# Two of GpSimd's weight differences put behind VectorE's short chains, alpha moved into the mix's addition, and experts 0 and 1 written out of the loop

## The chip, the cores and the metric

The program runs on one NeuronCore of one Trainium2 chip. The time is device microseconds (us) of that core, from the start to the end of the program on the chip. The kernel before was timed three times on its own: 1068.28 us is the median (1068.08 to 1070.03). A change is called faster or slower in this document only where it moves the median by over 0.2%.

## The reference

Two post-norm layers act on 512 tokens of 1024 channels in fp32. Each layer is a mix and a mixture of experts:

```
x <- LN(alpha * x + Mix(x))     # conv 256 channels | attention, 8 heads, chunks of 64 | gated MLP 256
x <- LN(alpha * x + MoE(x))     # 16 experts, 2 per token, SwiGLU of 512

h   = x @ w_in + b_in                                     # 1792 columns
c   = silu(LN(causal_conv31(a * sigmoid(g))))
att = softmax over the own and the previous chunk of 64 keys, with a learned sink per head
gm  = u * (masked 128x128 mixing of LN(v)) ,  u, v = gelu(h[...])
Mix = concat(c, att, gm) @ w_out + b_out
MoE = sum over the two chosen experts e of gate_e * (silu(x @ w_gate[e]) * (x @ w_up[e])) @ w_down[e]
```

alpha is (2 * 2) ** 0.25, the same number in both layers.

## The kernel before, in words

Every weight and every activation that TensorE multiplies is split into two numbers of TensorE's fast fp32 format, a high part and a low part, and each product is three matmuls: high by high, low by high and high by low. ScalarE makes the high part of a weight (a copy into `wh`), and VectorE or GpSimd makes the low part (`wl` = raw weight minus `wh`).

**The mix.** The weights of the mix come in 11 pieces a layer. Pieces 0 to 6 are the columns of `w_in`, pieces 7 to 10 are `w_out`. A piece is loaded by SyncE into one of two raw buffers, then ScalarE's `piece` (line 893) writes its high part into one of three slots, then a low part follows. Pieces 2 to 9 have their lows on GpSimd (`piece_lows`, line 1607), piece 10 on VectorE (line 1142). Piece 10's low part is the one that TensorE needs last, in the middle of `out_second`. SyncE loads piece q only when the low part of piece q - 2 is done, so a late low part also makes a late load.

VectorE meanwhile computes the convolution as 62 taps (line 1173), with the rotary products between them (`rope`, lines 1148 to 1150), then masks the score banks (line 1493), and then runs four short softmax chains, one for each block of 128 tokens: `softmax_max` (lines 1191 to 1197) before ScalarE's exponentials (lines 987 and 989), `softmax_norm` (lines 1204 to 1206) behind them. The probabilities are normalised in `Pm`, and TensorE turns them (`turn_probs`, line 597), scores the next block (`scores`, line 577) and multiplies by the values (`attend`, line 612). The order on each engine is written out by hand, and each waits for the others by semaphores, instruction by instruction.

GpSimd's queue in the mix is, in this order: the lows of pieces 2 to 7, a clear and two small transfers for the values (lines 1697 to 1699), four multiplications of the token-major input `xtok` by alpha (line 1706), the two powers for the norms (lines 1709 and 1711), the gated MLP's norm (line 1716), the lows of pieces 8 and 9, and four additions of `b_out` to `xtok` (line 1723). After that VectorE adds the projection to `xtok` (`add_mix`, line 1266) and takes the norm's sums.

**The experts.** The tokens are routed on the chip into chunks of 128 slots, one or more for each expert. TensorE runs one loop over all chunks. ScalarE, VectorE and GpSimd need to know which of the two weight buffers a chunk uses, so they run a loop over eight pairs of experts, and in it a loop for the chunks of each of the two (`chunk_loops`, lines 267 to 275). Each pass of the outer loop reads the experts' first chunks into registers (`first_chunk`, line 256). VectorE enters it right after `late_out` (line 1423), which waits for TensorE's `late_tables`. In every chunk VectorE first makes low parts of the gathered tokens (`gathered_low`, line 1142 with `xTl`), and then those of the first half of the gate weights; TensorE's `widen` (line 776) waits for both. `narrow` (line 794) is the down projection.

## Time and profile before

| | |
|---|---|
| median of three timed runs | 1068.28 us (1068.08 to 1070.03) |
| the profiled execution's own time | 1068.19 us |
| its span, first to last instruction | 1066.3 us |
| PE busy | 985.3 us (92%) |
| DVE busy | 809.4 us (76%) |
| ACT busy | 655.1 us (61%) |
| POOL busy | 539.8 us (51%) |
| chain that ended last | PE 69%, DVE 21%, issue 3%, POOL 2%, ACT 2% |
| mean over the DMA engines | 252 GB/s |

PE is TensorE, DVE VectorE, ACT ScalarE, POOL GpSimd and SP SyncE. The span has five parts: the first mix up to about 180 us, routing to 205, the experts of layer 0 to 525, the second mix to 720, and from 744 on the experts of layer 1 and the last norm. In the profile's lines "idle before" names what the engine waited for. PEclk is the share of full speed that TensorE was granted: 1.00 is 2.4 GHz, 0.50 is 1.2 GHz.

### The profile page before, as it was taken

How to read it: one execution, taken by the hardware profiler on the slowest of the kernel's cores; microseconds unless marked ns; L12 is line 12 of the kernel's file. 1: busy time of each engine (PE TensorE's matmuls, PEld its weight loads, DVE VectorE, ACT ScalarE, POOL GpSimd, SP SyncE). 2: the span in 40 equal slices, each digit the busy share in tenths (PEclk: the TensorE clock that was granted, in tenths of full speed). 3: DMA queues.
4: the chain of work that ended last, by engine and by line, in shares of the span. 5: the costliest groups of instructions: out<-in, count | busy, mean ns of one | idle time of the engine just before them, and what ended most of it. 6: DMA issues, size and time to landing. Idle time of an engine off the chain costs nothing.

```text
span 1066.3 us, 15510 instructions
## 1 busy us (share of the span) xinstructions
PE 985.3 (92%) x4852; PEld 792.6 (74%) x4852; DVE 809.4 (76%) x967; ACT 655.1 (61%) x737; POOL 539.8 (51%) x291
## 2 busy tenths in 40 slices
PE   7989998599999999999999979995999999999995
PEld 5876777488888888877778757774788888888882
DVE  5996757777878787777878977476877777777876
ACT  5324823377888787777533346323788787887861
POOL 1635354246566665545425354540656565656553
PEclk9998999599999999999999999996899999999998
DMA  9634293399999999995813211733999999999962
GB/s 291 222 89 174 69 335 125 134 318 354 359 346 367 342 333 342 354 344 174 251 53 119 79 49 40 291 143 116 324 372 362 360 365 360 356 362 333 368 218 82
DMA packets 122304, 268.51 MB, mean 252 GB/s; under 512 B 10523, under 2 KB 26043, under 8 KB 121760
## 3 DMA queue, kind: packets, MB, share of 16 engines
q1 hardware_dynamic: 111136, 247.14, 64.3%
q0 software_dynamic: 11136, 20.96, 7.4%
q8 instruction: 18, 0.29, 0.1%
q14 instruction: 14, 0.11, 0.0%
HBM read 259.19 MB, written 27.79 MB: 269 GB/s over the span
## 4 chain that ended last, share of the span: by engine, by line
PE 69%; DVE 21%; issue 3%; POOL 2%; ACT 2%; DVEq 1%; DMA 0%; SPq 0%; ACTq 0%
PE bank L776 34%; PE bank L794 17%; PE bank L431 9%; DVE bank L1173 7%; PE bank L754 2%; DVE xTl L1142 2%; POOL xtok L1621 1%; PE bank L748 1%; DVE moemem L1429 1%; DVE w_gate L1149 1%; PE bank L577 1%; DVE small L1194 1%; PE bank L829 1%; PE bank L825 1%; PE bank L544 1%
## 5 line engine op out<-in xcount | busy, mean ns | idle before, releaser
L1675 POOL TENSOR_TENSOR wl<-w_down,wh 128x2048 fp32r<-128x2048 f32 x33 | 151.8, 4601 | 148.8 <-ACT wh L1041 148.8
L1142 DVE TENSOR_TENSOR wl<-w_gate,wh 128x2048 fp32r<-128x2048 f32 (+1 forms) x75 | 169.5, 2260 | 53.1 <-ACT wh L1041 35.9
L1142 DVE TENSOR_TENSOR wl<-w_up,wh 128x2048 fp32r<-128x2048 f32 x66 | 151.2, 2293 | 29.2 <-ACT wh L1041 28.4
L1041 ACT ACTIVATE wh<-w_up 128x2048 fp32r<-128x2048 f32 x66 | 126.6, 1918 | 31.7 <-PE bank L794 21.7
L1041 ACT ACTIVATE wh<-w_down 128x2048 fp32r<-128x2048 f32 x66 | 126.7, 1920 | 31.0 <-PE bank L776 29.0
L776 PE MATMUL bank<-wl,xTh 128*128 128x512 f32 x528 | 144.0, 395 | 1.6 <-DVE wl L1142 1.6
L776 PE MATMUL bank<-wh,xTl 128*128 128x512 f32 x528 | 144.0, 395 | 1.1 <-DVE xTl L1142 1.1
L776 PE MATMUL bank<-wh,xTh 128*128 128x512 f32 x528 | 144.5, 396 | 0.2 <-ACT wh L1041 0.2
L1607 POOL TENSOR_TENSOR wl<-w_gate,wh 128x2048 fp32r<-128x2048 f32 x16 | 73.6, 4606 | 123.1 <-ACT wh L893 122.8
L1041 ACT ACTIVATE wh<-w_gate 128x2048 fp32r<-128x2048 f32 x66 | 126.5, 1916 | 12.8 <-PE bank L794 8.8
L1142 DVE TENSOR_TENSOR xTl<-bank,xTh 128x512 fp32r<-128x512 f32 (+1 forms) x168 | 89.8, 574 | 44.9 <-issue 21.4
L776 PEld LDWEIGHTS bank<-wl,xTh 128*128 128x128 f32 x528 | 100.1, 191 | 24.4 <-DVE wl L1142 3.9
L776 PEld LDWEIGHTS bank<-wh,xTl 128*128 128x128 f32 x528 | 100.6, 191 | 23.4 <-DVE xTl L1142 2.5
L776 PEld LDWEIGHTS bank<-wh,xTh 128*128 128x128 f32 x528 | 101.1, 192 | 21.7 <-issue 0.5
L431 PE MATMUL bank<-xTh,wh 128*128 128x512 f32 (+1 forms) x256 | 102.6, 401 | 11.2 <-DVE xTl L1142 9.8
L1654 POOL DMA_INDIRECT moemem<-x_rows,gather_idx x33 | 83.2, 2522 | 28.9 <-POOL gather_idx L1648 28.9
L431 PE MATMUL bank<-xTl,wh 128*128 128x512 f32 (+1 forms) x256 | 96.0, 375 | 0.0
L431 PE MATMUL bank<-xTh,wl 128*128 128x512 f32 (+1 forms) x256 | 95.9, 374 | 0.0
L1662 POOL DMA_INDIRECT y_rows<-moemem,scatter_idx x33 | 62.0, 1878 | 46.9 <-issue 46.9
L1142 DVE TENSOR_TENSOR wl<-w_down,wh 128x2048 fp32r<-128x2048 f32 x33 | 75.7, 2293 | 9.2 <-ACT wh L1041 8.3
L1173 DVE SCALAR_TENSOR_TENSOR bank<-w_down,col,bank 128x512 f32<-128x512 f32 x116 | 77.7, 748 | 1.7 <-DVE w_down L1157 0.5
L1045 ACT ACTIVATE xTh<-bank 128x512 fp32r<-128x512 f32 x66 | 39.1, 593 | 63.5 <-PE bank L748 63.5
(228 smaller groups left out, 1796.7 us busy)
## 6 DMA issues: line engine op xcount, KB each, us to landing
w_up<-in_exp_w_up SPq DMA_DIRECT2D x32, 2048.0 KB, 18.4
w_down<-in_exp_w_down SPq DMA_DIRECT2D x32, 2048.0 KB, 17.7
w_gate<-in_exp_w_gate SPq DMA_DIRECT2D x32, 2048.0 KB, 17.6
w_gate<-in_w_in SPq DMA_DIRECT2D x13, 1024.0 KB, 5.6
w_gate<-in_w_out SPq DMA_DIRECT2D x8, 1024.0 KB, 5.0
y_rows<-moemem SPq DMA_DIRECT2D x8, 512.0 KB, 9.4
x_rows<-xtok POOLq DMA_DIRECT2D x8, 512.0 KB, 3.0
w_up<-y_rows SPq DMA_DIRECT2D x8, 512.0 KB, 4.7
```

The lines of the kernel that those rows point to most:

```text
L431: mm = pe.matmul(out, xs[i], ws[k], start=(first and n == 0), stop=(last and n == 2))
L754: mm = pe.transpose(bank[4 + 3 * i][:, P * (k % 2):P * (k % 2) + P], sg[:, P * k:P * k + P], ident)
L776: mm = pe.matmul(bank[piece][:, :], xgT[m][:, 4 * (i % 2) + k, :], w[q][:, k, :], start=(i % 2 == 0 and n == 0 and k == 0), stop=(i % 2 == ...
L794: mm = pe.matmul(bank[5 + n][:, :], heT[m][:, 2 * (i % 2) + k, :], w[q][:, k, 512 * n:512 * n + 512], start=(i == 4 and t == 0 and k == 0) ...
L1041: act.activation(wh[s][:, :], slot[r][p][:, cols], ACT.Copy).then_inc(half_high, 1)
L1045: act.activation(xgT[0][:, 4 * i:4 * i + 4, :], bank[2 + i][:, :].rearrange("p (k t) -> p k t", k=4), ACT.Copy).then_inc(xgT_high, 1)
L1142: return dve.tensor_tensor(out, src, high.bitcast(F32), ALU.subtract)
L1173: y = dve.scalar_tensor_tensor(o, x, wk, o, ALU.mult, ALU.add)
L1607: pool.tensor_tensor(wl[(n + l) % SLOTS][:, :], wraw[n % 2], wh[(n + l) % SLOTS][:, :].bitcast(F32), ALU.subtract)\
L1654: pool.indirect_dma_start(xg, None, x1d[l], bass.IndirectOffsetOnAxis(ap=rows[:, :], axis=0), bounds_check=T - 1, oob_is_err=False).then_i ...
L1662: pool.indirect_dma_start(yd[l], bass.IndirectOffsetOnAxis(ap=scatter_idx[:, :], axis=0), ysb, None, bounds_check=T - 1, oob_is_err=False, ...
L1675: pool.tensor_tensor(wl[s][:, :], slot[r][p][:, cols], wh[s][:, :].bitcast(F32), ALU.subtract)\
```

## The change

There are three edits, all in the order or the form of instructions; TensorE's and SyncE's programs stay as they were.

1. GpSimd waits for `mask_set` (VectorE has masked the score banks) before the low part of piece 7, and for the second block's `pn_done` (its probabilities are normalised) before the low part of piece 8.
2. The four multiplications by alpha are gone. VectorE's `add_mix` computes x * alpha + projection in one instruction. So that `b_out` keeps its weight, GpSimd multiplies the row of `b_out` by 1 / alpha once, before its four additions.
3. `chunk_loops` runs experts 0 and 1 ahead of the loop over pairs, which starts at pair 1. The three first chunks are read before `late_out`'s wait on VectorE, and before the waits for the tables on GpSimd.

```diff
-        def chunk_loops(eng, l, body):
-
-            with eng.Fori(0, E // 2) as pair:
+        def chunk_loops(eng, l, body, ready=None):
+
+            starts = [first_chunk(eng, l, e) for e in range(3)]
+            if ready:
+                ready()
+            for r in range(2):
+                with eng.Fori(starts[r], starts[r + 1]) as c:
+                    body(c, 0, r)
+            with eng.Fori(1, E // 2) as pair:
...
-                link(dve.tensor_tensor(x, x, bank[4 * n + j][:, :], ALU.add))
+                link(dve.scalar_tensor_tensor(x, x, ALPHA, bank[4 * n + j][:, :], ALU.mult, ALU.add))
...
-                late_out(l)
-                chunk_loops(dve, l, lambda c, pair, r: chunk(l, c, pair, r))
+                dve.wait_ge(start_set, l + 1)
+                chunk_loops(dve, l, lambda c, pair, r: chunk(l, c, pair, r), lambda: late_out(l))
...
+                pool.wait_ge(mask_set, l + 1)
                 piece_lows(l, 7)
...
-                if l == 0:
-                    pool.wait_ge(xtok_in, 16)
-                else:
-                    pool.wait_ge(tr_done, TT * 2 * l)
-                for j in range(TT):
-                    link(pool.tensor_scalar(xtok[:, j, :], xtok[:, j, :], ALPHA, None, ALU.mult))
...
+                pool.wait_ge(pn_done, TT * l + 2)
                 piece_lows(l, 8)
                 piece_lows(l, 9)

                 pool.wait_ge(rows_in, 32 * l + 16)
+                link(pool.tensor_scalar(rows3[:, 0, :], rows3[:, 0, :], 1.0 / ALPHA, None, ALU.mult))
+                if l == 0:
+                    pool.wait_ge(xtok_in, 16)
+                else:
+                    pool.wait_ge(tr_done, TT * 2 * l)
                 for j in range(TT):
                     pool.tensor_tensor(xtok[:, j, :], xtok[:, j, :], rows3[:, 0, :], ALU.add).then_inc(xb_done, 1)
...
-                pool.wait_ge(tab_set, l + 1)
-                pool.wait_ge(late_set, l + 1)
-                chunk_loops(pool, l, lambda c, pair, r: chunk(l, c, r))
+
+                def tables():
+                    pool.wait_ge(tab_set, l + 1)
+                    pool.wait_ge(late_set, l + 1)
+
+                chunk_loops(pool, l, lambda c, pair, r: chunk(l, c, r), tables)
```

GpSimd in the mix of layer 0, before: the lows of pieces 3 to 7 (`wl<-w_gate,wh`), the values' transfers, alpha, the powers, the gated MLP's norm and the low of piece 8.

```order
L1607 TENSOR_TENSOR wl<-w_gate,wh 128x2048 [waits piece_high] x5
L1697 MEMSET w_down 64x128 [waits v_set]
L1698 DMA w_down<-w_down 64x512 [waits pool_chain]
L1699 DMA w_down<-w_down 64x384
L1706 TENSOR_SCALAR xtok<-xtok 128x1024 [waits xtok_in]
L1706 TENSOR_SCALAR xtok<-xtok 128x1024 [waits pool_chain] x3
L1709 TENSOR_TENSOR small<-small 128x4 [waits cvar_set,pool_chain]
L1711 TENSOR_TENSOR small<-small 128x4 [waits gvar_set]
L1716 TENSOR_TENSOR w_gate<-w_gate,w_down 128x1024 [waits row_in,gvh_set]
L1716 TENSOR_TENSOR w_gate<-w_gate,w_down 128x1024 [waits pool_chain]
L1607 TENSOR_TENSOR wl<-w_gate,wh 128x2048 [waits pool_chain,piece_high]
```

The same stretch of GpSimd's queue in the changed kernel:

```order
L1613 TENSOR_TENSOR wl<-w_gate,wh 128x2048 [waits piece_high] x4
L1613 TENSOR_TENSOR wl<-w_gate,wh 128x2048 [waits piece_high,mask_set]
L1704 MEMSET w_down 64x128 [waits v_set]
L1705 DMA w_down<-w_down 64x512 [waits pool_chain]
L1706 DMA w_down<-w_down 64x384
L1709 TENSOR_TENSOR small<-small 128x4 [waits cvar_set]
L1711 TENSOR_TENSOR small<-small 128x4 [waits gvar_set]
L1716 TENSOR_TENSOR w_gate<-w_gate,w_down 128x1024 [waits row_in,gvh_set]
L1716 TENSOR_TENSOR w_gate<-w_gate,w_down 128x1024 [waits pool_chain]
L1613 TENSOR_TENSOR wl<-w_gate,wh 128x2048 [waits pool_chain,piece_high,pn_done]
```

The four alpha instructions are out of it, and two lows have one more semaphore each. Further on in the same queue, the low of piece 9 and what follows it, before:

```order
L1607 TENSOR_TENSOR wl<-w_gate,wh 128x2048 [waits piece_high]
L1723 TENSOR_TENSOR xtok<-xtok,w_gate 128x1024 [waits rows_in]
L1723 TENSOR_TENSOR xtok<-xtok,w_gate 128x1024 x3
L1616 TENSOR_TENSOR small<-small 128x1 [waits ln_var]
L1621 TENSOR_TENSOR xtok<-xtok,w_gate 128x1024 [waits ln_scaled]
```

The same in the changed kernel, where `w_gate<-w_gate` is the row of `b_out`, scaled:

```order
L1613 TENSOR_TENSOR wl<-w_gate,wh 128x2048 [waits piece_high]
L1723 TENSOR_SCALAR w_gate<-w_gate 128x1024 [waits rows_in]
L1729 TENSOR_TENSOR xtok<-xtok,w_gate 128x1024 [waits xtok_in,pool_chain]
L1729 TENSOR_TENSOR xtok<-xtok,w_gate 128x1024 x3
L1622 TENSOR_TENSOR small<-small 128x1 [waits ln_var]
L1627 TENSOR_TENSOR xtok<-xtok,w_gate 128x1024 [waits ln_scaled]
```

One instruction has come in between the low of piece 9 and the additions. VectorE at the entry to layer 0's experts, before (`gatef` is what `late_out` writes, `starti` holds the first chunks):

```order
L1423 TENSOR_REDUCE gatef<-bank 128x48 [waits late_done]
L269 UNCONDITIONAL_BRANCH
L269 ISA
L256 TENSOR_LOAD starti
L256 ISA x3
L256 TENSOR_LOAD starti
L256 ISA x2
L274 UNCONDITIONAL_BRANCH
L274 ISA
L1142 TENSOR_TENSOR xTl<-bank,xTh 128x512 [waits xgT_high]
```

And in the changed kernel:

```order
L256 TENSOR_LOAD starti [waits start_set]
L256 ISA x2
L256 TENSOR_LOAD starti
L256 ISA x2
L256 TENSOR_LOAD starti
L256 ISA x2
L1429 TENSOR_REDUCE gatef<-bank 128x48 [waits late_done]
L273 UNCONDITIONAL_BRANCH
L273 ISA
L1148 TENSOR_TENSOR xTl<-bank,xTh 128x512 [waits xgT_high]
```

The reads of the first chunks now stand ahead of the wait, and one loop's entry is left behind it.

## Rows read from the trace of the kernel before

**Rows 1.** The chain that ended last, layer 0 experts and layer 1 mix: start us, us.
```profile
248.36 10.90 PE bank L776 x48
...
650.93 4.18 DVE small L1194
```

**Rows 2.** VectorE by time, layer 0 mix: start us, us, engine, line, operation [idle before].
```profile
68.41 0.69 DVE L1149 TENSOR_TENSOR w_gate<-w_gate,w_down 128x512 f32<-128x512 f32 x1
...
74.66 0.90 DVE L1149 TENSOR_TENSOR w_gate<-w_gate,w_down 128x512 f32<-128x512 f32 x1
...
89.69 0.84 DVE L1204 TENSOR_TENSOR small<-small 128x8 f32<-128x8 f32 x1 [1.61 <-ACT w_up L989]
...
96.16 0.17 DVE L1194 SCALAR_TENSOR_TENSOR small<-small,col 128x8 f32<-128x8 f32 x1
...
111.56 4.20 DVE L1194 SCALAR_TENSOR_TENSOR small<-small,col 128x8 f32<-128x8 f32 x1
...
143.94 0.28 DVE L1142 TENSOR_TENSOR wrs<-moemem,wrs 128x128 fp32r<-128x128 f32 x1
...
149.07 4.27 DVE L1142 TENSOR_TENSOR wl<-w_gate,wh 128x2048 fp32r<-128x2048 f32 x1 [4.85 <-ACT wh L893]
```

**Rows 3.** ScalarE by time around the third block's softmax.
```profile
113.40 1.28 ACT L987 ACT_TABLE_LOAD   x1
...
116.12 0.21 ACT L987 ACTIVATE small<-small 128x8 f32<-128x8 f32 x1 [1.44 <-DVEq L1198]
```

**Rows 4.** TensorE by time, layer 0 mix.
```profile
117.90 1.10 PE L597 MATMUL bank<-cst,w_up 128*128 128x128 f32 x8 [1.15 <-DVE w_up L1206]
...
119.17 2.56 PE L577 MATMUL bank<-w_gate 64*64 64x128 f32 x32 [0.17 <-ACT w_up L989]
...
155.02 0.39 PE L431 MATMUL bank<-wh,xTh 128*128 128x512 f32 x1
```

**Rows 5.** GpSimd by time, layer 0 mix.
```profile
70.40 4.61 POOL L1607 TENSOR_TENSOR wl<-w_gate,wh 128x2048 fp32r<-128x2048 f32 x1 [8.09 <-ACT wh L893]
...
83.69 11.40 POOL L1706 TENSOR_SCALAR xtok<-xtok 128x1024 f32<-128x1024 f32 x4
...
111.12 4.61 POOL L1607 TENSOR_TENSOR wl<-w_gate,wh 128x2048 fp32r<-128x2048 f32 x1 [0.18 <-POOL w_gate L1716]
...
141.62 2.38 POOL L1723 TENSOR_TENSOR xtok<-xtok,w_gate 128x1024 f32<-128x1024 f32 x1
...
143.96 2.52 POOL L1723 TENSOR_TENSOR xtok<-xtok,w_gate 128x1024 f32<-128x1024 f32 x1
...
148.80 2.39 POOL L1723 TENSOR_TENSOR xtok<-xtok,w_gate 128x1024 f32<-128x1024 f32 x1
```

**Rows 6.** VectorE by time: an addition with a product, and a plain one.
```profile
20.75 0.75 DVE L1157 SCALAR_TENSOR_TENSOR w_down<-bank,col,w_down 128x512 f32<-128x512 f32 x1 [1.07 <-PE bank L431]
...
175.17 0.69 DVE L1266 TENSOR_TENSOR xtok<-xtok,bank 128x512 f32<-128x512 f32 x1 [1.57 <-PE bank L431]
```

**Rows 7.** VectorE by time: first experts of layers 0 and 1.
```profile
206.96 1.35 DVE L1142 TENSOR_TENSOR xTl<-bank,xTh 128x512 fp32r<-128x512 f32 x3 [1.80 <-issue]
...
224.02 1.35 DVE L1142 TENSOR_TENSOR xTl<-bank,xTh 128x512 fp32r<-128x512 f32 x3 [0.37 <-ACT xTh L1045]
...
243.27 1.35 DVE L1142 TENSOR_TENSOR xTl<-bank,xTh 128x512 fp32r<-128x512 f32 x3 [1.40 <-issue]
...
745.96 1.35 DVE L1142 TENSOR_TENSOR xTl<-bank,xTh 128x512 fp32r<-128x512 f32 x3 [1.53 <-issue]
```

**Rows 8.** TensorE by time, first chunk of layer 0.
```profile
207.71 2.08 PE L776 MATMUL bank<-wh,xTl 128*128 128x512 f32 x4 [0.70 <-DVE xTl L1142]
...
210.57 2.08 PE L776 MATMUL bank<-wl,xTh 128*128 128x512 f32 x4 [0.79 <-DVE wl L1142]
```

**Rows 9.** One stretch: us, busy (x) PE PEld DVE ACT POOL, PEclk, DMA, GB/s.
```profile
189.30:216.50 27.20, 17.45 (x64) 13.58 (x65) 20.34 (x53) 10.10 (x10) 7.09 (x4) 0.50 0.32 107
```

**Rows 10.** ScalarE by time, a late expert of layer 0.
```profile
465.25 1.92 ACT L1041 ACTIVATE wh<-w_gate 128x2048 fp32r<-128x2048 f32 x1 [1.95 <-DMA w_gate<-in_exp_w_gate]
```

## The prediction

> **What bounds the kernel now.** I read the chain of waits first, then the engines' rows in order of time at the three places that the change touches. TensorE carries 69% of the chain, mostly the experts, where its matmuls follow each other without a gap: 48 of them take 10.90 us, 0.227 us each [rows 1]. Nothing in the change makes those shorter. What can move is where the chain leaves TensorE. In the mix of each layer it goes through a scalar_tensor_tensor of VectorE on 128x8 numbers that takes 4.20 us in layer 0 and 4.18 us in layer 1 [rows 1, 2]; elsewhere the same instruction takes 0.17 us [rows 2]. It begins at 111.56, 0.44 us after GpSimd's low part of piece 8 (111.12, 4.61 us) and ends when that ends, at 115.73 [rows 5]. At the entry to the experts, TensorE waits 0.70 and 0.79 us for VectorE, which itself stood 1.80 us for no semaphore [rows 7, 8].
>
> **Edit 1, the low part of piece 8.** With it behind the second block's probabilities, VectorE's 4.20 us become 0.17, and its small instructions up to the normalised probabilities are 4.03 us earlier. TensorE doesn't get all of that. ScalarE is the next to be late: its exponentials of the third block began at 116.12 after a wait of 1.44 us, and the table load in front of them ends at 113.40 + 1.28 = 114.68 [rows 3]. So they can start 1.42 us earlier. TensorE's turn of block 1 waited 1.15 us for VectorE, and its scores of the last block waited for ScalarE [rows 4]; the latter now come 1.42 us earlier, and all that follows hangs on these two. Gain 1.42 us a layer, bounds 1.15 (if only TensorE's first wait goes) and 4.03. The moved low begins at about 117.90 - 4.03 = 113.9 and ends at 118.5. The next instructions of VectorE wait for ScalarE, which is free only when the exponentials end, just before the scores, now at 119.17 - 1.42 = 117.75; two of them read PSUM and come first, so by the time two operands in SBUF are read the low has ended, and I count nothing there. If this cover fails, what comes back is at most the overlap, under 1 us. SyncE's load of piece 10 waits for this low and comes 2.8 us later, still far ahead of its use, which is just before 149.07 [rows 2].
>
> **The low part of piece 7.** It began at 70.40 and ended at 75.01; VectorE's rotary product at 74.66 took 0.90 us against 0.69 without it [rows 2, 5]. Behind the mask, which follows the last rotary product, it meets only taps and copies that read PSUM. Gain 0.21 us a layer. The values' transfers behind it on GpSimd and SyncE's load of piece 9 come a few us later; TensorE needs the first only when it attends (behind the turn at 117.90 at the latest), and the second is needed after that. I bound this edit by -0.2 and +1.0 us, the latter if the copy of the turned values were held up to the low's end.
>
> **Edit 2, alpha.** The four multiplications took 11.40 us of GpSimd [rows 5]. They slow small instructions of VectorE, 0.84 us for one at 89.69, but TensorE has a whole group of projection matmuls to do at that time, so removing them gives nothing. VectorE's addition changes its form: 0.69 us plain, 0.75 with a product [rows 6]. Of the eight a layer only the last stands on the path, behind TensorE's last projection: a cost of 0.06 us, bounds 0 and 0.1. The scaling of `b_out` adds one GpSimd instruction, 11.40 / 4 = 2.85 us, before the four additions, and this is the one place that can cost. VectorE's low part of piece 10 starts at 149.07 and takes 4.27 us: it stands until the fourth addition ends, 148.80 + 2.39 = 151.19, and then needs 2.15. It is there at 153.34, TensorE needs it at 155.02 [rows 2, 4, 5]. In the same frame of time the additions now begin at 141.62 + 2.85 = 144.47, at 2.39 each, so the boundary between the second and the third is at 149.26, 0.2 us after VectorE asks. At such a boundary VectorE got in before: its small low at 143.94 ran 0.28 us where one addition ended (144.0), and the next one was longer, 2.52 us for 2.39 [rows 2, 5]. So I take it that the low runs from 149.26 to 151.4, earlier than before, and that the additions wait for it. The last `b_out` is then ready near 156.4, about when VectorE comes to it. Cost 0. If it gets in one boundary later it ends at 153.8, still in time; if only after all four (154.04), at 156.2, 1.2 us late.
>
> The page SBUF — State Buffer of the Trainium skill, section "Who interferes with whom" and the one on the two sides, has VectorE (with two SBUF inputs, or in a mode with two ports) and GpSimd share a port pair that is locked for a whole instruction. The 4.20 us agree. The 0.84 us at 89.69 don't: VectorE was let through at 90.53, in the middle of an alpha multiplication (89.4 to 92.2), where the rule would have held it to the end. By the rule the low of piece 10 waits for one addition only, which gives the sum below.
>
> **Edit 3, the written-out experts.** Before, two reads and two loop entries stood between `late_out` and VectorE's first instruction of the chunk: 1.80 us in layer 0, 1.53 in layer 1 [rows 7]. Now the reads are done during TensorE's `late_tables` and one entry is left. The row nearest to it is the step from expert 0 to 1, with one read and one entry, which leaves at most 0.37 us visible [rows 7]; I take 0.40. That gives 1.40 and 1.13 us, bounds 0 and 1.8. TensorE stood 0.70 + 0.79 = 1.49 us before its third group [rows 8], so it can follow by 1.40. From there it is bound by itself. The later entry, into the loop over pairs, gets two reads and two loop entries, as the first one had: up to 1.80 us for 1.40 now. A gap of 1.40 costs nothing at present, as the unbroken matmuls of the chain show [rows 1, 7], and the 0.4 more I take as hidden.
>
> **The sum.** Layer 0: 1.42 + 0.21 - 0.06 + 1.40 = 2.97 us. Layer 1: 1.42 + 0.21 - 0.06 + 1.13 = 2.70. Together 5.67 us. The profiled execution took 1068.19 us (span 1066.3 and 1.9 around it), 0.1 under the median of the runs, so the sum serves for both: 1062.5 us.
>
> **The clock.** TensorE's granted clock is at 0.50, that is 1.2 GHz, from 189.3 to 216.5, through routing (TensorE nearly idle) and most of the first chunk [rows 9]; four matmuls take 2.08 us in it. The experts start 2.97 us earlier. If the low stretch still ends at 216.5, TensorE does that time's work at half speed and keeps half of it, 1.5 us; in layer 1 likewise 1.35. If it ends earlier by more than the start does, as much is won. I take the mean, and 2.85 us on both sides for the range.
>
> **The rivals.**
> A. As above: 1062.5, own range 1060.5 to 1064.5. Chance 0.56.
> B. The low clock keeps half of what reaches the experts: 1062.5 + 2.85 = 1065.4. For it: the first chunk lies in the low stretch. Against: the stretch is set off by the idle time in routing, which moves along. 0.13.
> C. VectorE's low of piece 10 gets in only after all of GpSimd's additions: 1.2 us in each layer, 1064.9. For it: in both layers it has so far ended with the last addition. Against: 143.94. 0.08.
> D. The weights of layer 0 set its end. ScalarE waits 1.95 us for a gate load of a late expert [rows 10]. If the stream of loads doesn't move with the loop's entry, its 1.40 us are lost: 1063.9. 0.08.
> E. The change doesn't do what it says at its main place: the stall merely moves to the next small instruction of VectorE, because the low of piece 8 starts before the last of them. Then 2 x 1.42 goes: 1065.3. Against: the wait is for the last instruction of that chain. 0.05.
> F. Slower. The code of experts 0 and 1 stands twice in ScalarE's and VectorE's programs, and each entry into code that hasn't run costs a fetch. That gives three entries more a layer (experts 1, 2 and 3) with a gap x, of which 1.40 us is hidden. Edit 3's 2.53 us are then not won either, so 3.14 are left of the gain. From x = 1.40 + 3.14 / 6 = 1.9 us the kernel isn't faster, from 2.3 it is slower by over 0.2%; at 3 us it is 6 x 1.6 - 3.14 = 6.5 us slower, 1074.7. For it: the first entries, 1.80 and 1.53, are longer than the repeated one. Against: the first entry into expert 1's code shows 0.37 [rows 7]. 0.10.
>
> The page Runtime: NRT & Kernel Launch of the Trainium skill, "Instruction fetch mechanics", says that instructions are prefetched in sequence and that a taken branch out of the fetched window stalls; it is the mechanism of F. No row here shows its price apart from the gaps named.
>
> **How the numbers follow.** 0.2% is 2.1 us, so faster means below 1066.1. A, B, C, D and E lie below, but B, C and E within 1.5 us of it, and errors of the terms add up: of their 0.90 I give 0.78 to faster, 0.11 to the same and 0.01 to slower. Of F's 0.10 I give 0.04 to the same and 0.06 to slower. The range goes from 1059.5 (A with the clock's other side) to 1067.0, and leaves out most of F.
>
> **What would show it.** Right: no short instruction of VectorE over 1 us in either mix behind piece 8's low; the exponentials of the third block start right behind the table load; the low of piece 10 takes under 3 us; VectorE's gap before the first chunk under 0.6 us; TensorE's matmuls unbroken from the second chunk on. The prediction is wrong if the two mixes end less than 1 us earlier, if TensorE waits in the middle of `out_second`, or if gaps appear between the first four experts.

## The result, and the profile after

The changed kernel takes 1057.07 us (median of 4 runs, 1056.84 to 1057.64), the kernel before on the same chip 1068.18 us (1067.48 to 1070.03). The ratio is 0.9896, with a 95% interval of 0.9881 to 0.9910: 11.1 us or 1.0% faster. The forecast was 1062.5 with a range of 1059.5 to 1067.0. The direction was right, but the gain is twice the 5.7 us of the sum, and the time lies 2.4 us below the range. The profiled executions show 10.5 us of it: their spans are 1066.3 and 1055.8 us. (One run of a kernel below, the one with TensorE's holes filled, took 4213 us for no reason seen here and is left out of its ratio.)

**VectorE in the third block's softmax**, layer 0, by time (start us, us, engine, line, operation, [idle before]), after:

```profile
111.83 0.17 DVE L1200 SCALAR_TENSOR_TENSOR small<-small,col 128x8 f32<-128x8 f32 x1
```

It took 4.20 us [rows 2]. In layer 1, where it took 4.18 [rows 1], no such instruction takes over 1 us either. It is not always 0.17: in five other profiles with edit 1 it takes 1.01 to 1.06 us, as in the second profile of the changed kernel:

```profile
110.72 1.04 DVE L1200 SCALAR_TENSOR_TENSOR small<-small,col 128x8 f32<-128x8 f32 x1
```

There the mix ran faster up to this point, and VectorE came while GpSimd's second instruction of the gated MLP's norm was running (109.33 to 111.73). ScalarE's table load began at 112.56, behind VectorE's chain, so here this cost nothing.

GpSimd's low parts of pieces 7 and 8, and further down its scaling of `b_out` and the four additions:

```profile
77.40 4.52 POOL L1613 TENSOR_TENSOR wl<-w_gate,wh 128x2048 fp32r<-128x2048 f32 x1 [14.82 <-DVEq L1500]
...
114.17 4.56 POOL L1613 TENSOR_TENSOR wl<-w_gate,wh 128x2048 fp32r<-128x2048 f32 x1 [3.00 <-DVE w_up L1212]
...
140.51 2.79 POOL L1723 TENSOR_SCALAR w_gate<-w_gate 128x1024 f32<-128x1024 f32 x1
143.39 11.53 POOL L1729 TENSOR_TENSOR xtok<-xtok,w_gate 128x1024 f32<-128x1024 f32 x4
```

Both lows are where the edit puts them. ScalarE and TensorE at the same place:

```profile
113.68 1.28 ACT L993 ACT_TABLE_LOAD   x1
114.98 0.21 ACT L993 ACTIVATE small<-small 128x8 f32<-128x8 f32 x1
```

```profile
116.95 1.09 PE L603 MATMUL bank<-cst,w_up 128*128 128x128 f32 x8
118.03 2.56 PE L583 MATMUL bank<-w_gate 64*64 64x128 f32 x32
```

The wait of 1.44 us behind the table load [rows 3] is gone. This execution runs 0.28 us later at this point (the load at 113.68, before at 113.40), and the scores start at 118.03 instead of 119.17 [rows 4]: 1.14 + 0.28 = 1.42 us, the forecast's number. (By its own rows the forecast should have had 116.12 - 114.68 = 1.44; 0.02 us stand between the load and the exponential.)

**VectorE at the end of the mix** and at the entry to the experts of layer 0:

```profile
147.96 2.34 DVE L1148 TENSOR_TENSOR wl<-w_gate,wh 128x2048 fp32r<-128x2048 f32 x1 [6.19 <-ACT wh L899]
150.22 0.68 DVE L1272 SCALAR_TENSOR_TENSOR xtok<-xtok,bank 128x512 f32<-128x512 f32 x1
...
203.45 0.26 DVE L1429 TENSOR_REDUCE gatef<-bank 128x48 f32<-128x96 f32 x1 [2.03 <-PE bank L746]
203.65 1.35 DVE L1148 TENSOR_TENSOR xTl<-bank,xTh 128x512 fp32r<-128x512 f32 x3
```

Piece 10's low part took 4.27 us [rows 2] and now takes 2.34: it ran at a boundary between two of GpSimd's additions, one of which waited, so that the four take 11.53 us instead of 4 x 2.39 (the third alone runs from 148.11 to 152.57). The addition with a product costs nothing over the plain one (0.68 us, 0.69 before [rows 6]). At the entry, where VectorE stood for 1.80 us [rows 7], there is no gap at all.

**TensorE at the entry** to the experts, after, first layer 0, then layer 1; the late tables are L746, and L782 is `widen`, a group of four matmuls a row:

```profile
201.47 1.94 PE L746 MATMUL bank<-wl,wh 128*128 128x96 f32 x8 [0.25 <-DVE wl L1424]
203.49 2.07 PE L782 MATMUL bank<-wh,xTh 128*128 128x512 f32 x4
205.35 1.73 PE L782 MATMUL bank<-wh,xTl 128*128 128x512 f32 x4
207.25 1.19 PE L782 MATMUL bank<-wl,xTh 128*128 128x512 f32 x4 [0.17 <-DVE wl L1148]
208.28 1.08 PE L782 MATMUL bank<-wh,xTh 128*128 128x512 f32 x4
...
733.96 1.95 PE L746 MATMUL bank<-wl,wh 128*128 128x96 f32 x8 [0.16 <-DVE wl L1424]
...
739.74 1.19 PE L782 MATMUL bank<-wl,xTh 128*128 128x512 f32 x4
```

The same places before that the rows ahead do not show:

```profile
202.92 1.30 PE L740 MATMUL bank<-wl,wh 128*128 128x96 f32 x5 [0.24 <-DVE wl L1418]
...
742.18 1.09 PE L740 MATMUL bank<-wl,wh 128*128 128x96 f32 x4 [0.15 <-DVE wl L1418]
...
749.57 0.80 PE L776 MATMUL bank<-wl,xTh 128*128 128x512 f32 x1 [0.79 <-DVE wl L1142]
```

From the tables to the third group it was 210.57 - 202.92 = 7.65 us [rows 8] and 7.39 in layer 1, and it is 5.78 in both. TensorE's holes in front of the second and the third group, 0.70 and 0.79 us in layer 0 [rows 8] and 0.35 and 0.79 in layer 1, have shrunk to one of 0.17 in layer 0. And a group takes about 1.08 us from 208.28 on, where it took 2.08 at 210.57 [rows 8]: the clock is back at its high level. The stretch from the third group to the end of the first chunk, before and after, both layers (windows: us, busy (x) PE PEld DVE ACT POOL, PEclk, DMA share, GB/s):

```profile
210.57:222.61 12.04, 12.04 (x41) 9.68 (x42) 9.53 (x5) 6.24 (x4) 4.46 (x3) 0.75 0.82 274
749.57:760.12 10.55, 10.55 (x41) 8.57 (x42) 9.53 (x5) 6.24 (x4) 4.46 (x3) 0.86 0.85 286
```

```profile
207.25:216.54 9.29, 9.29 (x40) 7.50 (x41) 8.83 (x5) 7.47 (x7) 3.39 (x3) 1.00 0.89 316
739.74:749.04 9.30, 9.30 (x41) 7.50 (x42) 8.84 (x5) 7.57 (x7) 3.34 (x3) 1.00 0.91 340
```

TensorE does the same work without a break in all four rows; 0.75 and 0.86 of full clock have become 1.00, and 12.04 and 10.55 us have become 9.3. The low level lasts from 186.3 to 206.7 here, 20.5 us; before it lasted from 189.3 to 216.6, 27.3 us [rows 9]. Where such a stretch ends is read from a window of half a microsecond in which the clock rises. A window at 0.76 has 0.24 us at the low level and the rest at the high one. The windows before, then after:

```profile
216.50:217.00 0.50, 0.50 (x3) 0.41 (x3) 0.50 (x1) 0.00 (x0) 0.00 (x0) 0.93 1.04 397
```

```profile
206.50:207.00 0.50, 0.50 (x2) 0.04 (x1) 0.50 (x1) 0.50 (x1) 0.50 (x1) 0.76 1.03 426
```

Where the 10.5 us of the two spans are, stage by stage. The rows above and [rows 8] give the marks; a layer runs here from `conv_mean`, the matmuls for the convolution's mean, to that of the next one or, at the end, to the addition of the experts' results:

```profile
82.63 2.08 PE L544 MATMUL bank<-w_up,onesc 128*128 128x512 f32 x2 [1.41 <-DVE w_up L1184]
622.40 2.62 PE L544 MATMUL bank<-w_up,onesc 128*128 128x512 f32 x3 [3.10 <-DVE w_up L1184]
...
1042.40 1.02 PE L829 MATMUL bank<-moemem 128*128 128x512 f32 x2
```

```profile
82.70 2.07 PE L550 MATMUL bank<-w_up,onesc 128*128 128x512 f32 x2 [1.42 <-DVE w_up L1190]
615.35 3.78 PE L550 MATMUL bank<-w_up,onesc 128*128 128x512 f32 x4 [1.40 <-DVE w_up L1190]
...
1031.90 1.88 PE L835 MATMUL bank<-moemem 128*128 128x512 f32 x4
```

| stage | layer 0 | layer 1 | both | forecast |
|---|---|---|---|---|
| `conv_mean` to the late tables | -1.52 | -1.17 | -2.69 | -3.14 |
| late tables to the third group | -1.87 | -1.61 | -3.48 | -2.53 |
| third group to the end of the first chunk (clock) | -2.75 | -1.25 | -4.00 | 0, at most 2.85 either way |
| second chunk (18.22 to 18.54, 18.21 to 18.51) | +0.32 | +0.30 | +0.62 | 0 |
| the rest | -1.30 | +0.28 | -1.02 | 0 |
| start, before `conv_mean` | +0.07 | | +0.07 | 0 |
| sum | | | -10.50 | -5.67 |

The line of the second chunk is part of the clock's price: with a faster first chunk TensorE catches up with VectorE and waits for it before the down projection, 0.50 us at 217.64 (for line 1435) where it waited 0.17 at 223.38 before. Two lines are not in the sum of the forecast: the clock, and 1.0 us in "the rest", which comes from the last four experts of layer 0 (76.54 us from one to the next in the profile before, 75.13 in the one after). The experiments are about these two.

### The profile page after: what moved, and what is told of

It reads as the page before. It is cut to its first block, busy times and chain, and to the rows that moved or that the text cites. A ratio compares the mean times of both kernels' runs of the same rounds, so it can differ in the third digit from the quotient of the medians.

```text
span 1055.8 us, 15474 instructions
## 1 busy us (share of the span) xinstructions
PE 983.2 (93%) x4852; PEld 791.2 (75%) x4852; DVE 790.0 (75%) x967; ACT 655.2 (62%) x737; POOL 530.6 (50%) x285
## 4 chain that ended last, share of the span: by engine, by line
PE 67%; DVE 19%; DMA 4%; SPq 4%; issue 3%; ACT 2%; DVEq 0%; ACTq 0%
PE bank L782 29%; PE bank L800 16%; PE bank L437 14%; DVE bank L1179 7%; SPq L340 4%; DMA w_up<-in_exp_w_up 2%; PE bank L760 2%; DVE xTl L1148 2%; PE bank L754 1%; DVE moemem L1435 1%; DMA moemem<-x_rows,gather_idx 1%; DVE w_gate L1155 1%; PE bank L835 1%; PE bank L831 1%; PE bank L550 1%
## 5 line engine op out<-in xcount | busy, mean ns | idle before, releaser
L1681 POOL TENSOR_TENSOR wl<-w_down,wh 128x2048 fp32r<-128x2048 f32 x33 | 154.1, 4669 | 143.0 <-ACT wh L1047 143.0
L1148 DVE TENSOR_TENSOR wl<-w_gate,wh 128x2048 fp32r<-128x2048 f32 (+1 forms) x75 | 166.9, 2226 | 51.6 <-ACT wh L1047 32.8
L782 PE MATMUL bank<-wh,xTh 128*128 128x512 f32 x528 | 143.2, 393 | 0.2 <-ACT wh L1047 0.2
L782 PE MATMUL bank<-wh,xTl 128*128 128x512 f32 x528 | 142.4, 392 | 0.0
L782 PE MATMUL bank<-wl,xTh 128*128 128x512 f32 x528 | 141.9, 391 | 0.3 <-DVE wl L1148 0.2
L1047 ACT ACTIVATE wh<-w_gate 128x2048 fp32r<-128x2048 f32 x66 | 126.5, 1916 | 11.9 <-PE bank L800 7.1
L782 PEld LDWEIGHTS bank<-wh,xTl 128*128 128x128 f32 x528 | 100.3, 190 | 21.1
L782 PEld LDWEIGHTS bank<-wh,xTh 128*128 128x128 f32 x528 | 99.9, 190 | 21.3 <-issue 0.5
L782 PEld LDWEIGHTS bank<-wl,xTh 128*128 128x128 f32 x528 | 98.6, 188 | 22.4 <-DVE wl L1148 2.1
L437 PE MATMUL bank<-xTh,wh 128*128 128x512 f32 (+1 forms) x256 | 102.9, 402 | 11.2 <-DVE xTl L1148 9.9
## 6 DMA issues: line engine op xcount, KB each, us to landing
w_gate<-in_exp_w_gate SPq DMA_DIRECT2D x32, 2048.0 KB, 19.2
```

Source lines behind the costliest of these rows:

```text
L437: mm = pe.matmul(out, xs[i], ws[k], start=(first and n == 0), stop=(last and n == 2))
L782: mm = pe.matmul(bank[piece][:, :], xgT[m][:, 4 * (i % 2) + k, :], w[q][:, k, :], start=(i % 2 == 0 and n == 0 and k == 0), stop=(i % 2 == ...
L1047: act.activation(wh[s][:, :], slot[r][p][:, cols], ACT.Copy).then_inc(half_high, 1)
L1148: return dve.tensor_tensor(out, src, high.bitcast(F32), ALU.subtract)
L1681: pool.tensor_tensor(wl[s][:, :], slot[r][p][:, cols], wh[s][:, :].bitcast(F32), ALU.subtract)\
```

## The experiments

Ratios are to the kernel before on the same chip, with their 95% intervals; a gain in us is the distance of the ratio from 1 times 1068.

**Edit 1 alone.** Only the two waits of GpSimd:

```diff
+                pool.wait_ge(mask_set, l + 1)
                 piece_lows(l, 7)
...
+                pool.wait_ge(pn_done, TT * l + 2)
                 piece_lows(l, 8)
```

> Edit 1 alone on the kernel before. Both theories: the 4.2 us stall of VectorE goes in both mixes, each mix ends 1.4 to 1.7 us earlier, and as the entry to the experts keeps its gaps of 1.80 and 1.53 us, the low clock in the first chunk stays nearly as it was: 3.0 us faster in all (1065.2). If the low clock's end were set by when the experts start (theory PLACE), the earlier start alone would already shorten the low stretch in the first chunk, and the kernel would be 6 us faster or more.

Measured: 1063.87 us, ratio 0.9956 (0.9932 to 0.9980), a gain of 4.7 us. The stall is gone from the mix; the third group still comes 7.65 and 7.38 us after the tables, and the low clock stretch in layer 0 is as long as before:

```profile
187.50:215.00 27.50, 17.82 (x65) 13.80 (x66) 20.67 (x52) 10.09 (x10) 7.10 (x4) 0.50 0.33 112
```

So the lows don't touch the clock at the entry. The gain is above the 3.0 us expected, with an interval (2.1 to 7.3) that holds it. The profiled execution, the slowest of the five, doesn't show the surplus: its span is 2.8 us shorter (1063.5), and from `conv_mean` to the late tables it gained 2.51 and 0.76 us, together 3.27. So where the other 1.7 us of the median come from isn't shown. How far one execution's mix can be trusted is. The window 97 to 110 us in the kernel before, then in this kernel:

```profile
97.00:110.00 13.00, 12.41 (x81) 10.72 (x81) 7.32 (x18) 6.85 (x21) 5.86 (x4) 0.87 0.00 1
```

```profile
97.00:110.00 13.00, 11.97 (x89) 10.43 (x87) 8.56 (x23) 8.40 (x22) 4.76 (x4) 1.00 0.12 47
```

The changed kernel has 0.87 in its first profile and 1.00 in its second. A second low stretch of the mix (100.5 to 103.9 before, 100.9 to 104.3 after) comes in some executions and not in others, whatever the kernel. The stage from `conv_mean` to the late tables took 118.77 us in the changed kernel with it and 117.25 without it. So one execution's mix is uncertain by 1.5 us a layer.

**Edit 2 alone.** Alpha out of GpSimd's queue into VectorE's addition:

```diff
-                    link(pool.tensor_scalar(xtok[:, j, :], xtok[:, j, :], ALPHA, None, ALU.mult))
...
-                link(dve.tensor_tensor(x, x, bank[4 * n + j][:, :], ALU.add))
+                link(dve.scalar_tensor_tensor(x, x, ALPHA, bank[4 * n + j][:, :], ALU.mult, ALU.add))
```

> Edit 2 alone. Both theories: no change within 0.2%. VectorE's low of piece 10 gets in between GpSimd's additions, TensorE waits nowhere in out_second, the first blocks' softmax is earlier without moving TensorE. If alpha's part were behind the unexpected gain, this would be over 1 us faster.

Measured: 1066.65 us, ratio 0.9985 (0.9972 to 0.9997), 1.6 us faster, under the 0.2% that this document calls a change. Nothing is lost, as forecast; whether anything is won is not settled. Its low part of piece 10 takes 2.33 us in both layers, at a boundary between GpSimd's additions, as in the changed kernel.

**Edit 3 alone.** Experts 0 and 1 written out, the first chunks read during the late tables:

```diff
+            starts = [first_chunk(eng, l, e) for e in range(3)]
+            if ready:
+                ready()
+            for r in range(2):
+                with eng.Fori(starts[r], starts[r + 1]) as c:
+                    body(c, 0, r)
```

> Edit 3 alone. Theory WORK (TensorE's clock rises once it works without holes, and the hole at the entry kept it low): the entry gains 1.9 and 1.6 us, and the low stretch ends several us earlier in the first chunk of both layers, worth 2.4 and 0.9 us more: 6.5 to 8 us faster. Theory PLACE (the clock's end moved because the experts start earlier by edit 1 and 3 together, or by chance): 3.5 us faster.

Measured: 1062.99 us, ratio 0.9948 (0.9930 to 0.9966), a gain of 5.6 us. The third group is 5.78 and 5.77 us behind the tables, and the low stretch in layer 0 lasts 20.5 us:

```profile
189.80:210.50 20.70, 12.45 (x54) 10.07 (x55) 15.88 (x51) 8.16 (x9) 3.73 (x3) 0.51 0.22 77
```

Nothing ahead of the entry is earlier here, and the clock's part comes whole with this edit. The gap itself is worth 3.5 us in two layers, which leaves 2.1 for the clock; in its profile the stretches from the third group to the chunk's end are 2.35 and 0.71 us shorter than before (9.69 and 9.84 us). The interval of the gain (3.6 to 7.5) leaves out PLACE's 3.5 narrowly and holds only the low end of WORK's 6.5 to 8: in kind it is WORK, in size less. The mean granted clock of the timed runs rises too, 0.9630 against 0.9611 before, where edits 1 and 2 alone have 0.9606 and 0.9610. The three edits alone add up to 4.7 + 1.6 + 5.6 = 11.9 us, the whole change to 11.1.

**A gap put back.** The changed kernel, with eight tiny memsets on VectorE behind `late_out`:

```diff
+            def entry(l):
+
+                late_out(l)
+                for _ in range(8):
+                    link(dve.memset(pad[:, :], 0.0))
```

> The changed kernel with eight tiny linked memsets (1.6 to 2 us) on VectorE between late_out and the first chunk, so that the gap of before is back and all else is as changed. Theory WORK: slower than the changed kernel by the gap in both layers and by what the low clock takes, 3.5 + 3.3 = 6 to 7 us (1063.5). Theory PLACE: slower by the gap alone, 3.5 us (1060.6).

Measured: 1061.77 us, ratio 0.9933 (0.9909 to 0.9956): of the 11.1 us, 3.9 are lost. The gap is 1.18 us (0.95 + 0.23), shorter than planned. VectorE, then TensorE:

```profile
202.47 0.95 DVE L1436 MEMSET pad<- 128x1 f32 x8
203.64 1.35 DVE L1149 TENSOR_TENSOR xTl<-bank,xTh 128x512 fp32r<-128x512 f32 x3 [0.23 <-DVE pad L1436]
```

```profile
207.25 2.07 PE L783 MATMUL bank<-wl,xTh 128*128 128x512 f32 x4 [0.78 <-DVE wl L1149]
209.12 1.88 PE L783 MATMUL bank<-wh,xTh 128*128 128x512 f32 x4
210.82 1.09 PE L783 MATMUL bank<-wh,xTl 128*128 128x512 f32 x4
```

Counted from the late tables (200.28 here) the third group comes after 6.97 us, 1.19 later than in the changed kernel, and TensorE has stood for 0.78 us in front of it instead of 0.17. The low clock lasts until 210.8, 10.6 us after the tables instead of 5.3, and the chunk's rest takes 10.88 us instead of 9.29, in layer 1 11.08 instead of 9.30. By the gap alone (PLACE) the kernel would lose twice 1.19, 2.4 us; with the clock of this profile 3.4 more, less the 0.6 of the second chunk, 5.1. The 3.9 measured lie between, and their interval (about 1.4 to 6.4, from this kernel's alone) decides nothing; the rows fit WORK. The five runs differ by more than is usual, 1060.11 to 1064.71, and the profiled one is among the slow ones (1063.52): that the clock is late in all of them isn't shown.

**TensorE kept busy in routing.** The kernel before, with matmuls whose results nobody reads:

```diff
+                keep_busy(24)
                 pe.wait_ge(rt_sel, l + 1)
...
+                keep_busy(12)
                 for q in range(2 * TT):
```

> The kernel before, with 36 matmuls of 128x512 on TensorE whose results nobody reads: 24 in routing, ahead of the wait for the ranks, and 12 ahead of the late tables; so TensorE is no longer nearly idle between the last projection and the experts. No instruction of the change is in it. CLOCK (the low stretch through the first chunk is set off by TensorE's idle time in routing, and what the first chunk loses is the price of it): the granted clock of the first chunk is 1.0 from its start or soon after, its period falls from 21.9 and 20.1 us to about 17 or less in both layers, and the kernel is 5 to 8 us faster than before, less what the added matmuls delay the routing (each 0.22 us at full clock, hidden as long as TensorE waits there). PLACE (the stretch is tied to something else, for example to the load on the chip at the experts' entry): the low stretch stays near 27 us, and the kernel is not faster.

Measured: 1065.39 us, ratio 0.9970 (0.9953 to 0.9987), 3.2 us faster, below the 5 to 8 that CLOCK expected. The low stretch does shrink, from 27.3 to 13.7 us, but from its front: it begins at 198.8 instead of 189.3 and still reaches to 212.5, past TensorE's holes at the entry, which this kernel still has. The tables come 0.9 us sooner a layer. From the third group to the chunk's end it takes 10.86 us in layer 0 and 11.08 in layer 1 (12.04 and 10.55 before), so that the entry gains little over both. So work in routing moves the start of the low stretch; what decides its end is still open here.

**The same in the changed kernel.**

> The changed kernel with the same 36 added matmuls in routing. CLOCK: its first chunks still have 20.7 us of low clock, most of it in routing where it costs little; what lies in the experts is about 3 us of work at half speed a layer, so it gains less than the kernel before does from them: 2 to 4 us, to about 1054, and ends close to the kernel before with them less 6 us. PLACE: no gain, 1057 or, with the added matmuls in the way, 1058 to 1060.

Measured: 1056.83 us, ratio 0.9874 (0.9848 to 0.9901); the changed kernel on the same chip 1057.70 and 0.9890 (0.9860 to 0.9919). No gain that can be told, where CLOCK expected 2 to 4 us. The 12 matmuls at the low clock are in the way of the tables, which come 0.9 us later, and there are two low stretches of 7 us instead of one of 20.5. From the third group to the chunk's end it takes 9.69 and 9.70 us, within what the changed kernel shows without them (9.29 to 10.03).

**The low part of piece 8 alone.** The second wait of edit 1 without the first.

> Edit 1 with the low part of piece 8 alone: the low part of piece 7 stays in front of the mask, alpha and the loop as before. By the terms of the forecast: 1.42 us a layer, 2.84 faster than before, and edit 1 whole should be 0.4 us better than this. RIVAL (the low part of piece 7 is what counts in edit 1): the kernel is within 1 us of before and most of the 5 us that edit 1 alone measured is missing.

Measured: 1064.33 us, ratio 0.9955 (0.9935 to 0.9974), 4.8 us, the same as edit 1 whole. The low of piece 8 carries the edit; the 0.42 us forecast for piece 7 are too little to be seen in times, though the rotary product at 74.94 took 0.69 us after instead of 0.90 [rows 2].

**The changed kernel again.**

> The changed kernel once more, on the same chip as the runs with the added matmuls, so that they are compared directly, and as a second profile of it: does the shorter stall of TensorE in the last experts of layer 0 repeat? If it belongs to the change, the last four periods of layer 0 sum to about 75.1 us again (77.6 - 1 before); if it is chance from one execution to the next, it moves by 1 us or so. Time expected 1057 (1056.5 to 1058).

Measured: 1057.70 us, ratio 0.9890 (0.9860 to 0.9919). The last four periods of layer 0 (from one chunk to the next) sum to 75.76 us, not 75.13; before they were 76.54, not the 77.6 of the expectation. The low clock reached 1.4 us into the third group this time, to 207.5:

```profile
206.10:215.98 9.88, 9.88 (x40) 8.05 (x41) 9.42 (x5) 7.56 (x7) 3.40 (x3) 0.93 0.91 338
738.23:748.26 10.03, 10.03 (x41) 8.20 (x41) 9.53 (x5) 7.67 (x7) 3.34 (x3) 0.91 0.86 313
```

That is 2.2 and 0.5 us less than before instead of 2.75 and 1.25, and here the second chunk takes 18.23 us in both layers. The clock's gain at the entry is thus 2.7 to 4.0 us, and net of what the second chunk gives back, 2.7 to 3.4.

**Only TensorE's holes filled.** The kernel before, with three unread matmuls between the late tables and the first chunk. Nothing else is changed, VectorE keeps its gap:

```diff
                 late_tables(l)
+                for k in range(3):
+                    pe.matmul(bank[0][:, :], xparts[0][:, 3 + k, 0:P], xparts[0][:, 3 + k, :], start=True, stop=True)
```

> The kernel before with three matmuls of 128x512 on TensorE between the late tables and the first chunk (1.56 us at the low clock), whose results nobody reads. VectorE keeps its gap of 1.80 and 1.53 us at the entry, the third group cannot start earlier than before, but TensorE no longer stands still for 0.70 and 0.79 us in front of the second and the third group. HOLE (the low clock lasts because TensorE stands still at the entry): the third group starts where it did, 0.1 us later at most, but the low stretch ends some 7 us earlier, as in edit 3 alone, and the first chunk's period falls by 2.5 to 3.5 us in each layer: 5 to 7 faster than before although nothing else is earlier. ELSEWHERE (the stretch's end has another cause, such as VectorE's or ScalarE's activity): the first chunk is as long as before, and the kernel is the same or 0.2 us slower.

Measured: 1065.68 us, ratio 0.9974 (0.9963 to 0.9985), a gain of 2.8 us. VectorE's gap is there, and TensorE's rows read:

```profile
208.91 1.35 DVE L1144 TENSOR_TENSOR xTl<-bank,xTh 128x512 fp32r<-128x512 f32 x3 [1.81 <-issue]
```

```profile
204.87 1.94 PE L740 MATMUL bank<-wl,wh 128*128 128x96 f32 x8 [0.25 <-DVE wl L1420]
206.61 1.61 PE L869 MATMUL bank<-xTh 128*128 128x512 f32 x3
208.02 1.91 PE L776 MATMUL bank<-wh,xTh 128*128 128x512 f32 x4
209.72 2.01 PE L776 MATMUL bank<-wh,xTl 128*128 128x512 f32 x4
212.52 1.19 PE L776 MATMUL bank<-wl,xTh 128*128 128x512 f32 x4 [0.79 <-DVE wl L1144]
```

The third group is 212.52 - 204.87 = 7.65 us behind the tables, exactly as before. One hole is filled (0.70 us before the second group), the other is still there, as 0.79 us. The low clock ends at 211.7, 6.9 us after the tables instead of 13.7, just as the remaining hole begins (211.73); in layer 1 it ends 6.2 us after them instead of 10.3:

```profile
211.50:212.00 0.50, 0.23 (x1) 0.00 (x0) 0.50 (x1) 0.49 (x1) 0.50 (x1) 0.78 1.06 426
```

From the third group to the chunk's end:

```profile
212.52:221.80 9.28, 9.28 (x41) 7.49 (x41) 8.82 (x5) 6.24 (x4) 4.46 (x3) 1.00 0.74 247
748.82:758.10 9.28, 9.28 (x40) 7.49 (x41) 8.82 (x5) 6.24 (x4) 4.46 (x3) 1.00 0.82 287
```

9.28 us where the kernel before takes 12.04 and 10.55: 2.76 and 1.27 us, the clock's line of the table (2.75 and 1.25) without one useful instruction being earlier. Of it the second chunk gives back 0.32 a layer here too (18.54), which leaves 3.4 us, and the times show 2.8. It is in the timed runs too: their mean granted clock is 0.9614 in 17 runs of the kernel before (0.960 to 0.963) and 0.9645 in 11 of this one (0.962 to 0.968). This is the clock that the sum lacked, without the change. HOLE holds; its size in time (5 to 7) was twice what there was to win.

**A smaller gap.** The changed kernel with three memsets instead of eight.

> The changed kernel with three tiny memsets of VectorE behind its late work instead of eight: a gap of about 0.4 us (eight gave 1.18), which is the residual gap of 0.40 us that the forecast had assumed. HOLE: the third group is 0.3 us later than in the changed kernel; if that is enough for the clock to stay low the 7 us longer, the kernel is 3 to 4.5 slower than the changed one, near 1061; if it isn't, it is 0.5 to 0.8 slower, near 1058. PLACE (what counts is only how early the work starts): in proportion to the gap, 0.8 slower, without a jump.

Measured: 1060.48 us, ratio 0.9930 (0.9915 to 0.9945). The third group is 0.56 us later than in the changed kernel, with a hole of 0.71 us in front of it (208.38 to 209.09), and yet the third group finds the clock back:

```profile
209.09:218.41 9.32, 9.32 (x40) 7.50 (x41) 8.86 (x5) 7.02 (x6) 3.95 (x3) 1.00 0.90 313
741.58:750.86 9.28, 9.28 (x40) 7.49 (x41) 8.82 (x5) 7.11 (x6) 3.04 (x2) 1.00 0.91 324
```

The low stretch had ended at 208.1, before the hole began, as in the kernel above. So these two kernels don't show that a hole of 0.7 to 0.8 us is harmless while the clock is low; in the one with eight memsets it lies inside the low stretch (206.47 to 207.25), and there the stretch went on. In time this kernel is 3.6 us behind the changed one, which would be HOLE's slow case, while its rows are those of the fast case: the time is no evidence for either. Twice 0.56 is the entry. A further part is elsewhere. VectorE's gap at the entry into a pass of the loop over pairs is 1.60 us in layer 1 here (at 845.35), where the changed kernel has 1.38 (at 842.85). The three memsets are executed once a layer and not in this loop; they have shifted the code behind them, and the same jump takes 0.2 us longer each time. (That it is the place of the code is argued, not shown.) Every second chunk grows from 18.25 to about 18.37 us (once to 18.66), about 1 us over the layer. With eight memsets the gap is 1.49 to 1.53, and in layer 0 of the changed kernel, where nothing was added, it is 1.47 to 1.57. The rest, some 1.5 us, is not explained and lies within the two intervals; in the profile 1.24 us of the difference stand ahead of the first `conv_mean`, where the two kernels do the same. The experiments with memsets therefore price a gap too high, and their kernels' times are weaker evidence than their rows.

**The kernel before again.**

> The kernel before once more, for a second profile. If the stall of TensorE in the last four experts of layer 0 (periods 18.20, 20.20, 18.88, 19.26 in the first profile, 76.5 us together) belongs to the kernel, they sum to 76.5 again; if it is chance, to anything between 74.6 and 76.5, as in the profiles of the variants with the same loop. Its first chunks should take 21.9 and 20.1 us again and the low stretches 27.7 and 23.9.

Measured: 1068.50 us, a single run. The last four periods of layer 0 are 18.99, 18.68, 19.02 and 19.25, 75.94 us together. Over all fourteen profiles the sums lie between 74.65 (low part of piece 8 alone, which has the old loop) and 77.89 (the kernel below, with the new loop and many waits for loads). With the loop of before they are 74.65 to 76.54, with the new one 75.13 to 77.89. So the 1.4 us between the first two profiles are no more than chance brings. The stretch behind the third group came out the same in this second profile:

```profile
211.13:223.12 11.99, 11.99 (x41) 9.61 (x42) 9.54 (x5) 6.23 (x4) 4.45 (x3) 0.75 0.80 271
749.97:760.58 10.61, 10.61 (x41) 8.63 (x41) 9.53 (x5) 6.23 (x4) 4.47 (x3) 0.86 0.85 286
```

It isn't as steady as that in kernels with the same entry: with edit 2 alone it takes 10.67 us in layer 0, with edit 1 alone 11.36 in layer 1 (the table below has all).

**TensorE kept busy in routing, other counts.** The changed kernel with 29 and 8 unread matmuls instead of 24 and 12.

> The changed kernel with 29 added matmuls in front of the ranks and 8 in front of the tables (the first attempt had 24 and 12, and there the 12 were in the way of the tables by 0.9 us at the low clock). CLOCK: with routing filled without a delay the full clock holds through routing or returns before the experts, and the first chunk takes 16.5 to 17.3 us in both layers; 1.5 to 3 us faster than the changed kernel, about 1055. If the clock goes to its low level anyway during the small matmuls of routing, it is the same as the changed kernel, 1056.5 to 1058.

Measured: 1055.60 us, ratio 0.9880 (0.9864 to 0.9896). The low stretch in layer 0 is down to 6.8 us (198.4 to 205.2) and the tables come 9.74 us behind the ranks instead of 10.64, but the first chunks, counted from the turning of their first tokens (line 754 in the changed kernel) to the end of `widen`, take 17.33 and 17.99 us, no less than without (17.29 and 17.20, in the second profile 17.89 and 17.94), and not the 16.5 to 17.3 that CLOCK expected. The median is 1.5 us below the changed kernel's 1057.07, with one long wait for a load in the profiled execution (a period of 22.09 us in layer 0). It is the lowest median of all here; that it is better isn't shown, since the intervals of the ratios overlap.

**All profiles side by side.** Each layer of each profile has one entry to the experts. "Hole" is the longest time that TensorE stood still between the first and the third group while the clock was still low. Both layers, us:

| kernel | hole | clock back, after the tables | third group to the chunk's end |
|---|---|---|---|
| before | 0.79, 0.79 | 13.7, 10.3 | 12.04, 10.55 |
| before, again | 0.79, 0.79 | 13.6, 10.4 | 11.99, 10.61 |
| edit 1 alone | 0.79, 0.79 | 13.7, 12.0 | 12.04, 11.36 |
| low part of piece 8 alone | 0.79, 0.78 | 10.9, 12.0 | 10.76, 11.35 |
| edit 2 alone | 0.79, 0.79 | 10.8, 10.6 | 10.67, 10.74 |
| before, routing filled | 0.78, 0.79 | 11.2, 11.4 | 10.86, 11.08 |
| changed, eight memsets | 0.78, 0.78 | 10.6, 11.0 | 10.88, 11.08 |
| first hole filled | none | 6.9, 6.2 | 9.28, 9.28 |
| edit 3 alone | none | 6.9, 7.1 | 9.69, 9.84 |
| changed | none | 5.3, 5.3 | 9.29, 9.30 |
| changed, again | none | 7.2, 7.5 | 9.88, 10.03 |
| changed, three memsets | none | 5.3, 5.3 | 9.32, 9.28 |
| changed, routing filled (24, 12) | none, 0.29 | 6.8, 6.8 | 9.69, 9.70 |
| changed, routing filled (29, 8) | none | 5.3, 8.2 | 9.32, 10.18 |

In 14 entries with a hole of 0.78 or 0.79 us the clock is back 10.3 us after the tables at the earliest, in 14 without one 8.2 at the latest. A single such hole went with a late clock in both layers with eight memsets, and with the first hole taken away the clock was early in both. The two layers together take 21.4 to 23.4 us behind the third group with the hole and 18.6 to 19.9 without, on average 22.3 and 19.2. In the three kernels with a single hole (first hole filled, eight and three memsets) the sorting follows in part what came out, since it asks whether the clock was still low; the other 22 entries are sorted by what the kernel is, 12 against 10, with the same bounds. The pair of profiles with which this document began lies near the far ends of both.

## Why the prediction was wrong in its size, step by step

- **The low part of piece 8**: right. The 4.20 us became 0.17 (1.0 in five other profiles), ScalarE's table load was next, and the scores came 1.42 us earlier, as worked out.
- **The low part of piece 7**: the rotary product went from 0.90 to 0.69 us, 0.21 as forecast. Too small for the times.
- **The mix as a whole** gave 2.69 us in the profile pair for 3.14, and edit 1 alone 4.7 in its times. The second profile of the changed kernel has 1.5 us less in this stage, with the clock at 1.00. So this term is right within what an execution's clock leaves open.
- **Edit 2 and the low of piece 10**: the mechanism was right. VectorE got in at a boundary between two additions (147.96, 2.34 us) and an addition waited. The rule of the Trainium skill that the prediction cites (SBUF — State Buffer, "Who interferes with whom") says the same of this place. Of alpha the traces say two things: the instruction at 89.69 that the prediction gives against the rule is not alone, since a product of VectorE with two SBUF inputs took 1.22 us at 90.81, all inside an alpha multiplication (89.48 to 92.25) and as long as without one (1.23 at 112.87 after); but another at 84.93 took 1.64 us and ended at 86.57, with the first multiplication (86.54). The 0.06 us for the changed form aren't there (0.68 against 0.69), and rival C is out: the low part takes 2.34 us in both layers.
- **The entry**: right in kind, too small. The step that took a residual gap of 0.40 us from the row at 224.02 failed: the gap is 0. The 0.37 us of that row are put down to ScalarE (`ACT xTh`) [rows 7], so it didn't measure the entry. That is 0.80 of the 0.95 us that were missing here (3.48 for 2.53). TensorE's own 1.49 us of standing still was no upper bound either: in layer 0 the third group came 1.87 us earlier, with 2.78 and 2.86 us from group to group before and 1.86 and 1.90 after.
- **The clock**: this is the step that failed. It held that the low stretch either ends where it ended or moves with the start, and took the mean, 0. The end is no such constant. TensorE's work at the entry had two holes, of 0.70 and 0.79 us in layer 0 [rows 8], and with them the low clock lasts until 13.7 and 10.3 us after the tables (216.6, 752.5); without them it ends after 5.3 in both layers (206.7, 739.2). The holes stood in the prediction, priced at their own length. Their real price was 4.0 us more in this pair of profiles (3.4 net of the second chunk), above the 2.85 that the range allowed. The kernel with nothing but unread matmuls in the first hole shows that price by itself, 2.76 and 1.27 us. Part of the 4.0 is luck of the pair: the averages of the table are 3.1 us apart.
- **Rival B** (the clock keeps half) had the sign wrong. **Rival D** (the loads of layer 0 set its end) is out: what was won at the entry of layer 0 was still there at its end ("the rest" is 1.30 us shorter, not 1.40 longer), and the sums of the last four experts don't follow the loop. **Rival E** is out by the row at 111.83. **Rival F** (code entries) is out as a loss, since no gap appears between the first experts. Something of its kind exists in small: the same entry into the loop in layer 1 shows 1.38, 1.50 or 1.60 us in kernels that differ by no, eight or three memsets ahead of the experts. The page Runtime: NRT & Kernel Launch of the Trainium skill, "Instruction fetch mechanics", has a taken branch stall for code outside what was fetched; the gaps agree with that, but no run here separates it from other costs of the jump.
- **The range** was too narrow on its lower side: 1059.5 is the sum with the clock's 2.85, and leaves no room for an entry gap of zero. Of the 5.4 us between the 5.7 forecast and the 11.1 measured, the profiles give 3.4 to the clock, 1.0 to the entry and 1.0 to chance in the last experts, less 0.45 in the mix; the last 0.6 is between the profiles and the timed runs.

What stays open is the rule behind it. The same hole gives an end anywhere from 10.3 to 13.7 us after the tables, and no hole one from 5.3 to 8.2; the changed kernel alone has 5.3 in one profile and 7.2 and 7.5 in the other. Two kernels had the hole only after the clock had risen, one had it at 6.2 us after the tables, before. So whether a hole meets a low clock is in part chance. The runs don't say more than that unbroken work at the entry brings the clock back sooner.

## What to carry to other kernels

Look for short waits of TensorE in a stretch where it is at its low clock and about to get busy: they can cost about twice their length (here 3.1 us over two layers beside the 2.6 us that TensorE stood still), because the low clock goes on over the work behind them. Price such a wait by the whole low stretch behind it, and keep both ends in the range. Before a stage's difference between two profiles is explained, look at a second profile of the same kernel: here the mix moved by 1.5 us and the last experts by 0.6 from one execution to the next.
